# Hybrid decoder trunk on one core: combining the experts' rows on TensorE and VectorE, and computing the position tables during the router

## Chip, cores and metric

The kernel runs on one core of a Trainium2 chip. The time is that of one execution on the device, in microseconds (us). Median before the change: 1937.03 us of 3 runs (1935.52 to 1939.13).

## What is computed

A trunk of two layers over 512 tokens of 1024 float32 values: layer 0 is an RWKV-7 time mix and a mixture of experts, layer 1 a sparse attention (NSA) with a shared key/value side and position bias, and a second mixture of experts; then a last norm. The change touches the mixtures of experts and the bias tables. In words of the reference, cut:

```python
def hier_moe(h, ln_g, w_gr, b_gr, w_er, b_er, w1, w3, w2):
    xf = rms_norm(h, ln_g)
    ...            # one of 4 groups, then 2 of its 8 experts per token
    weight = grp_w * ew / jnp.sum(ew, -1, keepdims=True)
    ...
    # per expert: (silu(xb @ w1[e]) * (xb @ w3[e])) @ w2[e], hidden size 512
    y = zeros.at[buf_t].add(yb * buf_w)      # each token: weighted sum of two rows
    return y
# the caller adds y to h
table = rel_bias.reshape(REL_BUCKETS, G, HPG).transpose(1, 2, 0)
logits = q @ k * scale + table[:, :, rel_bucket(distance)]
```

## The kernel before

The engines run hand-written instruction streams, ordered by semaphores; each stream is in order. SBUF is one arena of twelve regions of 4096 floats per partition; `h`, the residual stream, is region 0, as four blocks `j` of 128 tokens.

**Experts.** `moe_loads` lets SyncE load each of 32 experts' weights, w13 (4 MB, L375) and w2 (2 MB, L380), into one of three slots of three regions, as soon as TensorE has left the slot. In layer 0, w13(1), w2(1) and w13(2) are issued when the output product of the time mix is done (`wo_mm`), and w2(2) after `h_rwkv` = 8, since its region 5 held `x_again` until then. The router (L1763 places the tokens, L1766 counts them, after VectorE's chain up to `two_hot`, L1142) gives each token two experts. An expert holds 64 rows: `gather` (16 matmuls with a one-hot matrix), `hidden` (16 matmuls of 512 columns), ScalarE's silu (L744), VectorE's product (L1223), `transpose_gated` (L1792), VectorE's copy (L1232), `result` (8 matmuls), ScalarE's copy to `yb` (L750), and GpSimd's indirect DMA of these rows to `y_rows` in DRAM (L513).

**Combine.** When the stores of all 32 experts have landed, GpSimd gathers for each block `j` and each of its two choices `c` the rows by eight indirect DMAs (L544) to `y_got`; `combine` lets VectorE add them, weighted, to `h` (L1269, two a block). Then a block's norm: ScalarE's square (L568), VectorE's variance (L882), ScalarE's root (L573), VectorE's reciprocal (L887) and scaling (L892), TensorE's eight transposes (`turn_block`, L1412), and copies with the gain by VectorE (`turned`, L898) and ScalarE (L579). After layer 0 the q projection follows (w_qg), the gate product, and the K/V units (w_kv). After layer 1 a last scaling (L1397) and the store of the output follow. Of an expert with more than 64 tokens, the rest goes through the overflow branch (`n_over`), which the profiled execution does not enter.

**Position tables.** After layer 0's experts TensorE computes the bias tables from one-hot buckets: 55 matmuls for `bias_c` and two for the reversed rows. ScalarE copies them out (L768 to L771); SyncE later writes the reversed rows 128-fold to `rev_bias` in DRAM (L444), ahead of the second compression weights cmp_v_w1 (L446), and reads them back as `bias_h`. All matmuls are recorded at the helper lines `mm` (L1404) and `transpose` by their own lines; a float32 matmul is two instructions in the trace, a transpose one.

```python
                if l == 0:
                    sp.wait_ge(sem("h_rwkv"), 8)
                w2(2)
```

## Time and profile before

| | |
|---|---|
| median of 3 runs | 1937.03 us |
| profiled execution | 1936.99 us |
| its span | 1935.2 us |
| TensorE busy | 1811.9 us (94%) |
| VectorE, ScalarE, GpSimd busy | 596.3, 360.5, 219.7 us |
| mean granted TensorE clock | 0.96 |
| DMA | 499.73 MB, mean 258 GB/s |

PE is TensorE, DVE VectorE, ACT ScalarE, POOL GpSimd, SP SyncE. PEclk is the granted clock of TensorE as a share of 2.4 GHz, so 0.50 is 1.2 GHz. Times inside the trace count from the span's start.

### The profile page before, as it was taken

The numbers are of one execution on the slowest core, as the hardware profiler recorded it, in microseconds if no ns is written. First come the engines' busy times: TensorE is split into PE (matmuls) and PEld (weight loads), VectorE is DVE, ScalarE is ACT, GpSimd is POOL, SyncE is SP. The second block draws the span as 40 slices with busy tenths as digits, with TensorE's granted clock in tenths as the row PEclk, the third lists the DMA queues.
The fourth block names the chain that finished last, engine by engine and source line by source line (L and its number), as shares of the span: only waits on it lengthen the run. The fifth ranks groups of instructions, "written<-read, shape, count | busy, mean of one in ns | idle before, by whom it ended". The sixth has DMA issues, their size and how long they took to land.

```text
span 1935.2 us, 25676 instructions
## 1 busy us (share of the span) xinstructions
PE 1811.9 (94%) x10954; PEld 956.7 (49%) x10954; DVE 596.3 (31%) x1269; ACT 360.5 (19%) x846; POOL 219.7 (11%) x264
## 2 busy tenths in 40 slices
PE   7989988989799999999969999999979999999993
PEld 3334347755554454445434577555554544454440
DVE  5462793452221111111140335564222111111113
ACT  2432113311100000000030123665210000000001
POOL 2044000000000000000020001453000000000002
PEclk9989998999799999999969999999979999999997
DMA  5112743060899999999959302010379999999994
GB/s 206 63 68 50 276 123 49 3 269 1 347 416 432 428 426 430 430 430 428 422 220 167 68 22 109 13 34 1 131 298 407 431 431 428 428 430 429 429 404 153
DMA packets 60930, 499.73 MB, mean 258 GB/s; under 512 B 28079, under 2 KB 28591, under 8 KB 42383
## 3 DMA queue, kind: packets, MB, share of 16 engines
q1 hardware_dynamic: 53391, 481.26, 62.1%
q0 software_dynamic: 7424, 16.80, 2.4%
q8 instruction: 89, 1.46, 0.3%
q14 instruction: 26, 0.21, 0.0%
HBM read 465.23 MB, written 41.18 MB: 262 GB/s over the span
## 4 chain that ended last, share of the span: by engine, by line
PE 84%; DVE 8%; issue 3%; DMA 3%; POOL 1%; ACT 1%; SPq 0%; POOLq 0%; DVEq 0%; ACTq 0%
PE bank L1404 71%; PE bank L1456 5%; PE bank L1987 3%; PE bank L2001 2%; DVE spare L1017 2%; DVE arena L1018 1%; PE bank L1792 1%; DVE arena L1269 1%; DMA arena<-y_rows,ints 1%; POOL arena L493 1%; DMA arena<-gram_dram 1%; POOL arena L491 0%; PE bank L1412 0%; DVE arena L1031 0%; PE bank L1564 0%
## 5 line engine op out<-in xcount | busy, mean ns | idle before, releaser
L1404 PE MATMUL bank<-arena 128*64 128x512 f32 (+8 forms) x5090 | 1255.8, 546 | 26.2 <-DVE arena L982 9.5
L1404 PEld LDWEIGHTS bank<-arena 128*64 128x64 f32 (+4 forms) x5090 | 482.6, 156 | 676.4 <-issue 653.3
L1404 PEld LDWEIGHTS bank<-const,arena 128*128 128x128 f32 x2048 | 238.9, 195 | 51.2 <-issue 48.7
L1404 PE MATMUL bank<-const,arena 128*128 128x128 f32 x2048 | 250.7, 282 | 2.2 <-DVE const L1148 2.2
L513 POOL DMA_INDIRECT y_rows<-arena,ints x64 | 63.1, 986 | 1124.4 <-ACT arena L750 923.5
L1223 DVE TENSOR_TENSOR arena<-arena,bank 128x256 f32<-128x256 f32 x64 | 27.0, 421 | 426.6 <-ACT arena L744 426.6
L750 ACT ACTIVATE arena<-bank 128x512 f32<-128x512 f32 x64 | 38.3, 598 | 424.2 <-PE bank L1404 424.2
L744 ACT ACTIVATE arena<-bank 128x256 f32<-128x256 f32 x64 | 24.6, 385 | 469.2 <-PE bank L1404 469.2
L1155 DVE TENSOR_TENSOR arena<-bank,vec 128x512 f32<-128x512 f32 x64 | 44.3, 692 | 193.3 <-PE bank L1404 193.3
L560 POOL TENSOR_SCALAR arena<-arena,small 128x128 f32<-128x128 f32 (+3 forms) x128 | 77.0, 612 | 143.7 <-DVE small L1381 143.2
L1232 DVE COPY arena<-bank 128x256 f32<-128x256 f32 x64 | 27.2, 424 | 184.3 <-PE bank L1792 184.3
L1456 PE MATMUL bank<-arena 128*64 128x64 f32 (+2 forms) x1760 | 65.9, 231 | 10.6 <-DVE arena L1031 5.4
L851 ACT ACTIVATE arena<-arena,small 128x128 f32<-128x128 f32 (+3 forms) x128 | 70.5, 552 | 25.9 <-DVE small L1373 25.8
L1456 PEld LDWEIGHTS bank<-arena 128*64 128x64 f32 (+2 forms) x1760 | 59.8, 143 | 17.1 <-DVE arena L1031 6.2
L1373 DVE CUSTOM_DVE_ANT_0 arena<-bank,arena 128x128 f32<-128x128 f32 (+3 forms) x128 | 58.0, 489 | 23.3 <-PE bank L1404 22.3
L1987 PE MATMUL bank<-const,arena 128*128 128x128 f32 x320 | 62.7, 294 | 0.7 <-POOL arena L560 0.6
L1987 PEld LDWEIGHTS bank<-const,arena 128*128 128x128 f32 x320 | 34.4, 140 | 40.3 <-POOL arena L560 24.6
L2001 PE MATMUL bank<-arena 128*64 128x128 f32 x640 | 49.1, 282 | 0.4 <-DVE arena L1388 0.4
L927 DVE SCALAR_TENSOR_TENSOR arena<-arena,vec 128x512 f32<-128x512 f32 x48 | 36.9, 797 | 39.4 <-PE bank L1404 34.9
L1388 DVE COPY arena<-bank 128x128 f32<-128x128 f32 (+3 forms) x64 | 31.1, 486 | 42.9 <-PE bank L1987 42.6
L1017 DVE TENSOR_TENSOR spare<-arena 128x529 f32<-128x529 f32 (+30 forms) x40 | 43.1, 1078 | 1.4
L2001 PEld LDWEIGHTS bank<-arena 128*64 128x64 f32 x640 | 33.9, 136 | 16.3 <-issue 9.3
(239 smaller groups left out, 981.5 us busy)
## 6 DMA issues: line engine op xcount, KB each, us to landing
arena<-m_w SPq DMA_DIRECT2D x64, 4096.0 KB, 18.5
arena<-m_w SPq DMA_DIRECT2D x64, 2048.0 KB, 17.2
y_rows<-state SPq DMA_DIRECT2D x1, 8192.0 KB, 22.6
arena<-kv_w SPq DMA_DIRECT2D x1, 6144.0 KB, 18.4
rev_bias<-arena SPq DMA_DIRECT2D x1, 5120.0 KB, 70.1
arena<-a_wk SPq DMA_DIRECT2D x2, 2048.0 KB, 15.1
arena<-a_wr SPq DMA_DIRECT2D x2, 2048.0 KB, 8.0
arena<-a_wv SPq DMA_DIRECT2D x2, 2048.0 KB, 8.0
```

The costliest lines, as they stand in the source:

```text
L513: nc.gpsimd.indirect_dma_start(out=y_halves, out_offset=bass.IndirectOffsetOnAxis(ap=store_i[:, e:e + 1], axis=0), in_=yb[:, n % 2, :], in ...
L560: nc.gpsimd.tensor_scalar(row, row, share[:, n % 4, i:i + 1], gates[:, j, g:g + 1], ALU.mult, ALU.mult).then_inc(sem("shared"), 1)
L750: nc.scalar.activation(yb[:, n % 2, :], bank[6 + n % 2][:, :], ACT.Copy).then_inc(sem("yb_ready"), 1)
L851: last = nc.scalar.activation(probs[:, n % 4, i, 0:P * (j + 1)], probs[:, n % 4, i, 0:P * (j + 1)], ACT.Exp, scale=-1.0, bias=top[:, n % 4 ...
L927: return nc.vector.scalar_tensor_tensor(dst[:, k, :], xxT[:, k, :], v8(f"mu{mu}")[:, k:k + 1], xT[:, k, :], ALU.mult, ALU.add)
L1017: solved(nc.vector.tensor_tensor(prod, known, below, ALU.mult))
L1155: nc.vector.tensor_tensor(xgT[:, n % 2, 4 * q:4 * q + 4, :], bank[2 + q][:, :].rearrange("p (k t) -> p k t", k=4), spread(gain[:, 4 * q:4 ...
L1373: last = nc.vector.tensor_tensor_reduce(out=probs[:, n % 4, i, 0:P * (j + 1)], in0=bank[2 * (n % 2) + i][:, 0:P * (j + 1)], in1=bias_h(m)[ ...
L1404: return nc.tensor.matmul(dst, lhsT, rhs, start=start, stop=stop)
L1456: return nc.tensor.matmul(dst, lhsT, rhs, start=start, stop=True, skip_group_check=True)
L1987: last = nc.tensor.transpose(bank[4 + i][:, P * s:P * s + P], probs[:, n % 4, i, P * s:P * s + P], ident)
L2001: last = nc.tensor.matmul(bank[6 + m % 2][64 * i:64 * i + 64, P * j:P * j + P], values[:, s, b, HD * (m // 2):HD * (m // 2) + HD], probs_T ...
```

## The change

- **The last two experts** (30 and 31) are not stored and gathered. VectorE writes, in expert 29 (`tail_picks`), weighted one-hot matrices of both; TensorE transposes them (`tail_turn`, eight transposes) within expert 30, ScalarE copies them to `tail_T`. After the last expert `tail_add(j)` multiplies them with `yb` in SBUF: four matmuls a block, each with 64 rows, into banks 2j and 2j + 1.
- **The other thirty** are gathered once the stores up to expert 29 have landed (`EARLY` = 30), to regions 3 and 4. VectorE sums them (`early_sum`), except for block 2 (layer 0) and blocks 1 and 2 (layer 1), where TensorE adds them with diagonal matrices (`early_add`, four matmuls). VectorE then adds both banks to `h`.
- **The position tables** of layer 0 are computed in the router, before the tokens are placed: SyncE loads buckets and `rel_bias` between w13(2) and w2(2), TensorE does four matmuls (three of 512 columns, one of 128) into 16 partitions, ScalarE copies, SyncE stores them to DRAM, and w2(2) waits for the store. `bias_c` is later read from there by eight DMAs, and `rev_bias` is written from DRAM.
- **The scaling** of the norm after layer 0 moves from VectorE to ScalarE. Weight slots are counted by `e % 3`; overflow has buffers of its own; several tiles change regions; w_qg is loaded in halves and w_kv in thirds.

The diff, cut to these parts:

```diff
@@ -392,6 +406,12 @@
                 w13(2)
                 if l == 0:
                     sp.wait_ge(sem("h_rwkv"), 8)
+                    sp.dma_start(fwd, d["bucket_fwd"]).then_inc(sem("bucket_in"), 16)
+                    sp.dma_start(rev, d["bucket_rev"]).then_inc(sem("bucket_in"), 16)
+                    sp.dma_start(rel[0:32, :], d["rel_bias"]).then_inc(sem("bucket_in"), 16)
+                    sp.wait_ge(sem("bias_ev"), at("bias_ev", 4))
+                    sp.dma_start(bias_dram, bias_rows).then_inc(sem("bias_out"), 16)
+                    sp.wait_ge(sem("bias_out"), at("bias_out", 16))
...
 
-            sp.wait_ge(sem("hidden_mm"), at("hidden_mm", E - 2))
-            sp.dma_start(w_qg[:, 0:7, :], d["b_wqg"][:, 0:7, :]).then_inc(sem("q_w_in"), 16)
-            sp.wait_ge(sem("expert_mm"), at("expert_mm", E - 2))
-            for i in range(2):
-                sp.dma_start(fwd[i], d["bucket_fwd"]).then_inc(sem("bias_in"), 16)
-                sp.dma_start(rev[i], d["bucket_rev"]).then_inc(sem("bias_in"), 16)
-                sp.dma_start(rel[i][0:32, :], d["rel_bias"]).then_inc(sem("bias_in"), 16)
-            sp.dma_start(w_qg[:, 7, :], d["b_wqg"][:, 7, :]).then_inc(sem("q_w_in"), 16)
+            sp.wait_ge(sem("hidden_mm"), at("hidden_mm", E - 1))
+            sp.dma_start(w_qg[:, 0:4, :], d["b_wqg"][:, 0:4, :]).then_inc(sem("q_w_in"), 16)
+            sp.wait_ge(sem("expert_mm"), at("expert_mm", E - 1))
+            sp.wait_ge(sem("y_got1"), 32)
+            sp.dma_start(w_qg[:, 4:NK, :], d["b_wqg"][:, 4:NK, :]).then_inc(sem("q_w_in"), 16)
             overflow_sp(0)
             sp.wait_ge(sem("combined"), 8)
-            sp.dma_start(w_kv, d["kv_w"]).then_inc(sem("kv_w_in"), 16)
+            for i in range(3):
+                sp.dma_start(w_kv[i], d["kv_w"][:, i, :, :]).then_inc(sem("kv_w_in"), 16)
+            for a in range(8):
+                sp.dma_start(bias_c[16 * a:16 * a + 16, :, :],
+                             bass.AP(tensor=bias_dram.tensor, offset=9 - a, ap=[[64, 16], [1664, NH], [1, NOFF]])
+                             ).then_inc(sem("bias_c_in"), 16)
             sp.dma_start(cmp_w1[0], d["cmp_k_w1"]).then_inc(sem("cmp_w1_in0"), 16)
             sp.dma_start(cmp_w2[0], d["cmp_k_w2x2"].rearrange("(s p) n -> p s n", p=P)).then_inc(sem("cmp_w2_in"), 16)
             sp.dma_start(cmp_w2[1], d["cmp_v_w2"].rearrange("(s p) n -> p s n", p=P)).then_inc(sem("cmp_w2_in"), 16)
             for i in range(2):
                 sp.dma_start(cmp_pe[i], d["pe_k" if i == 0 else "pe_v"]).then_inc(sem("cmp_pe_in"), 16)
-            sp.wait_ge(sem("rev_ev"), at("rev_ev", 1))
-            sp.dma_start(rev_dram, spread(rev_rows, 1, P)).then_inc(sem("rev_out"), 16)
+            sp.dma_start(rev_dram, spread(bias_dram[:, 1024:1664], 1, P)).then_inc(sem("rev_out"), 16)
             sp.wait_ge(sem("gate_mm"), at("gate_mm", 1))
...
                         bounds_check=2 * SLOTS - 1, oob_is_err=False).then_inc(sem(f"y_store{n % 2}"), 16)
 
                 pool.wait_ge(sem("entries_ready"), at("entries_ready", l + 1))
+                for i in range(2):
+                    pool.wait_ge(sem(f"y_store{i}"), 16 * (EARLY // 2) * (l + 1))
+                pool.wait_ge(sem("hidden_mm"), at("hidden_mm", E * l + EARLY))
+                for j in range(NJ):
+                    for c in range(2):
+                        nc.gpsimd.indirect_dma_start(
+                            out=y_got[:, j, c, :], out_offset=None, in_=y_rows,
...
                 nc.scalar.activation(grp4, grp4, ACT.Exp).then_inc(sem("group_exp"), 1)
+                if l == 0:
+                    act.wait_ge(sem("bias_mm"), at("bias_mm", 4))
+                    for i, (a, b, sign) in enumerate(((0, 512, 1.0), (512, 1024, 1.0), (1024, 1536, -1.0), (1536, 1664, -1.0))):
+                        nc.scalar.activation(bias_rows[:, a:b], bank[(6, 7, 0, 1)[i]][0:NH, 0:b - a], ACT.Copy,
+                                             scale=sign).then_inc(sem("bias_ev"), 1)
                 act.wait_ge(sem("top_diff"), at("top_diff", l + 1))
                 nc.scalar.activation(e21, e21, ACT.Exp).then_inc(sem("top_exp"), 1)
...
                         nc.scalar.activation(yb[:, n % 2, :], bank[6 + n % 2][:, :], ACT.Copy).then_inc(sem("yb_ready"), 1)
+                        if e == EARLY - 1:
+                            for i in range(2):
+                                act.wait_ge(sem("tail_mm"), at("tail_mm", 2 * l + i + 1))
+                                nc.scalar.activation(tail_T[:, i, :, :].rearrange("p j t -> p (j t)"), bank[2 + i][:, :],
+                                                     ACT.Copy).then_inc(sem("tail_turned"), 1)
                 n_over = act.value_load(over_count, min_val=0, max_val=OVER)
                 with act.If(n_over > 0):
                     with act.Fori(0, n_over) as b:
...
             nc.scalar.activation(root_warm, gn_eps, ACT.Sqrt)
             for j in range(NJ + 2):
                 if 1 <= j <= NJ:
                     norm_root(2, j - 1)
+                    act.wait_ge(sem("norm_rstd"), 4 * 2 + j - 1 - 3)
+                    nc.scalar.activation(xn_m[:, j - 1, :], h[:, j - 1, :], ACT.Copy,
+                                         scale=rstd[:, j - 1:j]).then_inc(sem("xn_ready"), 1)
                 if j < NJ:
```

```diff
+                def tail_picks():
+                    for c, hot in enumerate((hot1, hot2)):
+                        to = tail_f if c else tail_w
+                        then(nc.vector.tensor_tensor(to, hot[:, :, EARLY:E], spread(combine_w[:, :, c], 2, 2), ALU.mult))
+                    then(nc.vector.tensor_tensor(tail_w, tail_w, tail_f, ALU.add))
+                    dve.wait_ge(sem("gathered_T"), at("gathered_T", 32 * (l + 1)))
+                    for i in range(2):
+                        tile = one_hot[:, i, :, :, :]
+                        then(nc.vector.tensor_tensor(tile, spread(spread(cst("iota")[:, 1:CAP + 1], 1, 2), 1, NJ),
+                                                     spread(spread(place_of[:, :, EARLY + i], 2, 2), 3, CAP), ALU.is_equal))
+                        nc.vector.tensor_tensor(tile, tile, spread(spread(tail_w[:, :, i], 2, 2), 3, CAP),
+                                                ALU.mult).then_inc(sem("tail_hot"), 1)
+                    lo = by_pe[l][0]
+                    n = 2 * len(by_pe[l])
+                    nc.vector.tensor_tensor(early_diag[:, 0:n, :], spread(ident, 1, n),
+                                            spread(small[:, 464 + 2 * lo:464 + 2 * lo + n], 2, P), ALU.mult).then_inc(sem("diag_ready"), 1)
 
                 dve.wait_ge(sem("place_mm"), at("place_mm", l + 1))
...
+
+            early_sums = [0]
+
+            def early_sum(l, j):
                 dve.wait_ge(sem(f"y_got{j}"), 32 * (l + 1))
                 for c in range(2):
-                    if c:
-                        dve.wait_ge(sem("combined"), 8 * l + 2 * j + 1)
-                    nc.vector.scalar_tensor_tensor(h[:, j, :], y_got[:, j, c, :], combine_w[:, j, c:c + 1], h[:, j, :],
-                                                   ALU.mult, ALU.add).then_inc(sem("combined"), 1)
+                    nc.vector.scalar_tensor_tensor(h[:, j, :], y_got[:, j, c, :], early_w[:, j, c:c + 1], h[:, j, :],
+                                                   ALU.mult, ALU.add).then_inc(sem("early_sum"), 1)
+                    early_sums[0] += 1
+                    dve.wait_ge(sem("early_sum"), at("early_sum", early_sums[0]))
+
+            def combine(l, j):
+                if j not in by_pe[l]:
+                    early_sum(l, j)
+                dve.wait_ge(sem(f"tail_out{j}"), at(f"tail_out{j}", l + 1))
+                for q in range(2):
+                    cols = slice(512 * q, 512 * q + 512)
+                    nc.vector.tensor_tensor(h[:, j, cols], bank[2 * j + q][:, :], h[:, j, cols],
+                                            ALU.add).then_inc(sem("combined"), 1)
 
             moe_dve(0)
...
                     combine(0, j)
                 if 1 <= j <= NJ:
                     norm_var(2, j - 1)
-                    norm_scale(2, j - 1)
+                    dve.wait_ge(sem("norm_std"), 4 * 2 + j - 1 - 3)
+                    nc.vector.reciprocal(rstd[:, j - 1:j], rstd[:, j - 1:j]).then_inc(sem("norm_rstd"), 1)
...
 
+                if l == 0:
+                    pe.wait_ge(sem("bucket_in"), at("bucket_in", 48))
+                    pe.wait_ge(sem("rel_mask"), at("rel_mask", 1))
+                    for b, table in ((6, fwd[:, 0:512]), (7, fwd[:, 512:1024]), (0, rev[:, 0:512]), (1, rev[:, 512:640])):
+                        mm(bank[b][0:NH, 0:table.shape[1]], rel, table).then_inc(sem("bias_mm"), 1)
                 pe.wait_ge(sem("two_hot"), at("two_hot", l + 1))
...
+
+                def tail_turn(i):
+                    pe.wait_ge(sem("tail_hot"), at("tail_hot", 2 * l + i + 1))
+                    for j in range(NJ):
+                        last = nc.tensor.transpose(bank[2 + i][:, P * j:P * j + P],
+                                                   one_hot[:, i, j, :, :].rearrange("p e t -> p (e t)"), ident)
+                    last.then_inc(sem("tail_mm"), 1)
+
+                def tail_add(j):
+                    for i in range(2):
+                        for q in range(2):
+                            rows = slice(CAP * q, CAP * q + CAP)
+                            last = mm(bank[2 * j + q][:, :], tail_T[rows, i, j, :], yb[rows, i, :], i == 0, i == 1 and j not in by_pe[l])
+                    if j not in by_pe[l]:
+                        last.then_inc(sem(f"tail_out{j}"), 1)
+
+                def early_add(j):
+                    pe.wait_ge(sem(f"y_got{j}"), 32 * (l + 1))
+                    for q in range(2):
+                        for c in range(2):
+                            last = mm(bank[2 * j + q][:, :], early_diag[:, 2 * by_pe[l].index(j) + c, :],
+                                      y_got[:, j, c, 512 * q:512 * q + 512], False, c == 1)
+                    last.then_inc(sem(f"tail_out{j}"), 1)
 
...
                     if e:
                         expert_result(e - 1)
+                    if e == EARLY:
+                        for i in range(2):
+                            tail_turn(i)
                     pe.wait_ge(sem("gated_ready"), at("gated_ready", n + 1))
+                    if n == 0:
+                        pe.wait_ge(sem("bias_ev"), at("bias_ev", 4))
...
+                tail_add(0)
+                if l == 0:
+                    tail_add(1)
+                    tail_add(3)
+                    tail_add(2)
+                    early_add(2)
+                else:
+                    tail_add(1)
+                    early_add(1)
+                    tail_add(2)
+                    early_add(2)
+                    tail_add(3)
 
             moe_pe(0)
 
-            pe.wait_ge(sem("bias_in"), at("bias_in", 96))
-            pe.wait_ge(sem("rel_mask"), at("rel_mask", 1))
-            for m in range(NOFF):
-                mm(bank[m % 2][:, 16 * (m // 2):16 * (m // 2) + 16], fwd[m % 2][:, 864 - 16 * m:992 - 16 * m], rel[m % 2])
-            mm(bank[3][0:NH, 0:128], rel[1], rev[1][:, 512:640])
-            mm(bank[2][0:NH, :], rel[0], rev[0][:, 0:512]).then_inc(sem("bias_mm"), 1)
-            pe.wait_ge(sem("rev_ev"), at("rev_ev", 1))
             for j in range(NJ):
                 turn_block(2, j, 2 * j)
```

## Rows read from the trace of the kernel before

**Rows 1.** Windows view; columns: stretch, length, busy (instructions) by engine, PEclk, DMA share, GB/s.

```profile
513.30:978.00 464.70, 464.14 (x2568) 221.01 (x2568) 66.75 (x154) 31.12 (x64) 30.60 (x31) 1.00 0.98 414
978.00:1011.00 33.00, 16.87 (x145) 13.53 (x143) 18.05 (x27) 12.97 (x37) 8.96 (x10) 0.57 0.55 203
```

**Rows 2.** Chain of waits, layer 0's last expert on; columns: start us, us, what.

```profile
974.03 3.68 PE bank L1404 x16
977.73 0.61 ACT arena L750
...
986.20 7.09 DMA arena<-y_rows,ints
...
1010.86 1.19 PE bank L1404
```

**Rows 3.** Chain of waits, the kernel's end.

```profile
1899.20 3.68 PE bank L1404 x16
...
1930.85 1.28 DVE arena L1397
```

**Rows 4.** Chain of waits, layer 0's router.

```profile
498.58 0.21 DVE spare L1142
...
502.29 10.28 PE bank L1404 x64
```

**Rows 5.** Source view of w13's load line, the load issued at 484.3.

```profile
L375 SPq DMA_DIRECT2D arena<-m_w x1: 432/432/432, 484.3 to 484.3; - x1
...
DMA to landing us min/median/max: 26.4/26.4/26.4
```

**Rows 6.** DMA issues of SyncE's queue, 405 to 413; columns: KB each, median us to landing.

```profile
arena<-x SPq DMA_DIRECT2D x1, 2048.0 KB, 12.2
...
state<-router_b SPq DMA_DIRECT2D x1, 36.0 KB, 12.0
```

**Rows 7.** Groups by form, 978 to 1011; columns: busy, mean ns | idle before.

```profile
L1269 DVE SCALAR_TENSOR_TENSOR arena<-arena,small 128x1024 f32<-128x1024 f32 x8 | 10.3, 1283 | 16.6 <-DMA arena<-y_rows,ints 16.5
L1412 PE MATMUL bank<-const,arena 128*128 128x128 f32 x32 | 7.8, 426 | 14.9 <-DVE arena L892 14.9
...
L579 ACT ACTIVATE arena<-bank,vec 128x128 f32<-128x128 f32 x18 | 5.0, 367 | 1.9 <-PE bank L1412 1.9
L898 DVE TENSOR_TENSOR arena<-bank,vec 128x512 f32<-128x512 f32 x7 | 4.5, 684 | 0.6 <-PE bank L1412 0.6
L568 ACT ACTIVATE arena<-arena 128x1024 f32<-128x1024 f32 x4 | 4.2, 1044 | 1.4 <-DVE arena L1269 1.4
...
L1404 PE MATMUL bank<-arena 33*16 33x512 f32 x2 | 1.9, 1044 | 0.0
...
L1404 PE MATMUL bank<-arena 33*16 33x128 f32 x2 | 0.6, 404 | 0.0
```

**Rows 8.** Windows view, short stretches for TensorE's granted clock.

```profile
502.00:506.00 4.00, 3.71 (x17) 3.71 (x18) 0.54 (x3) 0.00 (x0) 0.00 (x0) 0.50 1.06 459
...
508.00:509.00 1.00, 1.00 (x9) 1.00 (x9) 0.00 (x0) 0.00 (x0) 0.00 (x0) 0.84 1.06 459
...
982.00:984.00 2.00, 2.00 (x30) 2.00 (x29) 0.00 (x0) 0.00 (x0) 1.31 (x2) 0.69 0.00 0
```

**Rows 9.** The page's costliest groups, the gather's matmul.

```profile
L1404 PE MATMUL bank<-const,arena 128*128 128x128 f32 x2048 | 250.7, 282 | 2.2 <-DVE const L1148 2.2
```

**Rows 10.** Source view of the expert store's line, the store issued at 963.8.

```profile
L513 POOL DMA_INDIRECT y_rows<-arena,ints x1: 972/972/972, 963.8 to 963.8; - x1
...
DMA to landing us min/median/max: 10.8/10.8/10.8
```

**Rows 11.** TensorE groups by form, 1192 to 1389.

```profile
L1404 PE MATMUL bank<-arena 128*128 128x512 f32 x96 | 42.0, 593 | 0.0
L1404 PE MATMUL bank<-arena 64*128 64x512 f32 x64 | 18.1, 641 | 0.0
```

**Rows 12.** Windows view, the stretch in which rev_bias is broadcast.

```profile
1030.00:1050.00 20.00, 20.00 (x48) 8.76 (x48) 0.69 (x1) 1.19 (x2) 0.00 (x0) 1.00 0.95 100
```

More of the change, by code:

```diff
@@ L244, in decoder_program @@
         combine_w = small[:, 88:96].rearrange("p (j c) -> p j c", c=2)
+        early_w, over_w, tail_w = (small[:, 464 + 8 * i:472 + 8 * i].rearrange("p (j c) -> p j c", c=2) for i in range(3))
         slot_i = ints[:, 0:8].rearrange("p (j c) -> p j c", c=2)
+        over_slot_i = ints[:, 176:184].rearrange("p (j c) -> p j c", c=2)
+        is_early, tail_f = scratch(NJ * 2), scratch(NJ, 2)
         entry_i = ints[:, 8:16].rearrange("p (j c) -> p j c", c=2)
@@ L306, in decoder_program @@
         NU = len(UNITS)
-        final_gain = region(3)[:, 0:D]
+        final_gain = region(7)[:, 0:D]
         block = stack.enter_context(nc.Block())
@@ L509, in moe_pool @@
                 pool.wait_ge(sem("store_rows"), l + 1)
-                for e in range(E):
+                for e in range(EARLY):
                     n = E * l + e
@@ L1112, in moe_dve @@
                     add(j)
+                    if l == 0 and j == NJ - 1:
+                        dve.wait_ge(sem("h_rwkv"), 8)
+                        nc.vector.memset(rel[32:33, :], NEG).then_inc(sem("rel_mask"), 1)
                     norm_var(i, j)
@@ L1262, in moe_dve @@
                         dve.wait_ge(sem(f"over_store{l}"), 32 * b + 32)
-            def combine(l, j):
+                    dve.wait_ge(sem(f"over_got{l}"), 128)
+                    for j in range(NJ):
+                        for c in range(2):
+                            then_over(nc.vector.scalar_tensor_tensor(h[:, j, :], over_got[:, j, c, :], over_w[:, j, c:c + 1], h[:, j, :],
+                                                                     ALU.mult, ALU.add))
+            early_sums = [0]
```

188 lines of the change are left out of this document (104 added, 84 removed), and 2 rows, old and new, of the table GOES_ON.

## The prediction

> **What bounds the kernel now.** I read the busy time by stretches first [rows 1]. In the first mixture-of-experts stretch TensorE is busy 464.14 of 464.70 us at full clock. What the change can win or lose there shows only when TensorE itself gains work or waits. In the 33.00 us after it, which the stretch view shows from 978 to 1011, TensorE is busy only 16.87 us. The chain of waits says why [rows 2]: the last expert's matmuls start at 974.03 and end 3.68 us later (977.71), then come ScalarE's copy, the store of its rows, a gather that lands after 7.09 us, the sums and norms, and the q projection only at 1010.86. That is a gap of 33.15 us. At the end of the kernel it is the same [rows 3]: matmuls end at 1902.88, VectorE's last instruction at 1930.85 + 1.28 = 1932.13, 29.25 us later, and 3.07 us of output store follow. These two gaps are what the change attacks.
>
> The third place is the router before the first experts. There the chain goes through VectorE to TensorE: two_hot is written at 498.58 + 0.21 = 498.79, after which TensorE places the tokens and begins gathering at 502.29 [rows 4]. The change puts a wait and four matmuls of TensorE just ahead of that placing.
>
> **Part 1, the tables in the router's wait (layer 0).** SyncE now issues the three table loads after w13(2) and ahead of w2(2); they can't go earlier, since region 5 holds x_again until h_rwkv. I look at what stands ahead of them. w13(2) is issued at 484.3 and lands 26.4 us later, at 510.7 [rows 5], because w13(1) and w2(1), issued in the microsecond before, go first. Do small transfers pass large ones in this queue? Earlier, the router's 36 KB bias, issued behind the 2 MB reload of x, took 12.0 us, against x's own 12.2: it landed with the large one, 1/57 of its size [rows 6]. I read this as one queue in order. So the tables (132 + 82.5 + 2 KB, some 0.5 us at the stretch's 414 GB/s) land near 511.2. TensorE's new wait for bucket_in holds everything behind it in order: the placing, the first gather, the first expert. It could have gone on at 498.79, so the stall is 12.4 us. What VectorE's router chain hides (TensorE idle until 498.84) is already used up by then.
>
> Then come four table matmuls, on the path. Of this shape the old kernel ran one with 512 columns, two instructions in 1.9 us, and one with 128 columns, 0.6 us, both at the low clock [rows 7]; three and one cost 3 x 1.9 + 0.6 = 6.3 us. ScalarE's four evacuations are covered by placing and gathering (over 10 us); the store of the tables and its round trip only delay w2(2), which is needed two experts later, and w13(3) waits for the first expert anyway. Part 1 adds 12.4 + 6.3 = **18.7 us**. The 57 matmuls removed after the experts save nothing: they lay in the 33 us gap, which ended by the gather.
>
> Clock: it stood at 0.50 from 502 to 506, and rose within 508 to 509, under the wide gather matmuls; and within 982 to 984 it fell to a mean of 0.69 while TensorE was busy all the time with the old narrow table matmuls [rows 8]. So I count on no help from narrow matmuls. Bounds: nothing, or the gather of 10.28 us [rows 4] at full clock, where the 2048 of its form take 250.7 / 2048 = 0.122 us each, 64 of them 7.8 us [rows 9]: 2.5 us less. I take nothing.
>
> **Part 2, the combine after layer 0.** TensorE gains eight transposes for the tail (tail_turn), within expert 30: in this stretch eight take 7.8 / 4 = 2.0 us at the low clock [rows 7], half of it, 1.0, at full: **+1.0 us** a layer, since TensorE is the bound there. VectorE's picks fall into its idle time. The gathers move: the store of expert 29 starts about where one did before (963.8) and that one landed after 10.8 us beside weight loads [rows 10]; I let this one land by 971 to 975, since less is queued, and the eight gathers, an issue of about 1.3 us each, between 978 and 991. The w_qg half now waits for y_got1, is 2.2 MB, so about 5 us, and is there well before its use.
>
> From the last expert matmul (+0), the new chain: copy 0.6; tail_add(0), four matmuls with 64 rows, 64 instructions of that form take 18.1 us [rows 11], so 0.565 us a matmul, 2.26 in all: +2.9. VectorE adds two halves of block 0 at 0.69 each (a PSUM operand, 4.5 / 7 in the row, rounded up) [rows 7]: +4.3. TensorE goes on with three more tail_adds and early_add(2), four matmuls with 128 rows at 2 x 42.0 / 96 = 0.875: 2.9 + 6.8 + 3.5 = +13.1. VectorE's block 1 needs two sums (1.28 each) and two adds: +8.3. Block 2 waits for TensorE: +14.5. Then block 1's norm steps and a turned copy (1.3), two sums and two adds of block 3: +19.8. Now ScalarE, which has taken over the scaling, is last: per block a scaling (1.04, at its square's price), a square with its read (1.25), a turned copy (1.14): after scaling(2) +21.3, square(3) +22.6, turned(1) +23.7, scaling(3) +25.2; transposes at the low clock (2.0) +27.2, the last turned copy **+28.4**. Against 33.15 that gains 4.7 us, far less than the earlier landing of the rows: what the DMA no longer holds, VectorE's 19.8 us and then ScalarE do.
>
> **Part 3, the combine after layer 1.** TensorE: tail0 +2.9, tail1 and early1 +8.6, tail2 and early2 +14.3, tail3 +16.6. VectorE: block 0 +4.3, block 1 waits, +10.0, its neighbour's norm and final product (1.9) +11.9; block 2 waits, +15.7, final +17.6; block 3 with sums and adds (4.0) +21.6; two finals +25.2. Before 29.25: gain 4.0 us.
>
> **Other parts, at nothing.** Six more small operations in entries() (0.2 to 0.3 us each) lie under expert 4; renamed regions and slots keep the order of frees. The position table now reaches bias_c by DMA, and the broadcast to rev_bias reads DRAM. The old broadcast ran at 100 GB/s with the DMA 0.95 busy [rows 12], 5.24 MB in some 50 us, and cmp_v_w1 is queued behind it when the gate product is done; before its user, the second compression product, come six K/V units of 8 x 0.875 = 7.0 us, 42 us of slack. At the old rate it is hidden; if that cover goes, rival (d) has the price.
>
> **Sum.** 18.7 + 2 x 1.0 - 4.7 - 4.0 = +12.0 us. The profiled execution took 1936.99 us (span 1935.2; the rest lies around it), the median shown is 1937.03, the same. Forecast 1936.99 + 12.0 = **1949.0 us**, slower.
>
> **Rivals.**
> (a) The tables don't queue (the other side): the first table load is issued near 485; if it lands before 493, the 6.3 us of matmuls fill TensorE's idle 6.1 us ahead of 498.84 and Part 1 costs 0.2. Then 1936.99 + 0.2 + 2.0 - 8.7 = 1930.5 us. It decides if small transfers pass w13(1) to w13(2); against it stand the transfers of [rows 6]. The whole change breaks even at a landing near 499. 13%.
> (b) The table matmuls wake the clock. In rows: the 2.5 us of above come back, 1946.5 us. For: the clock rose under the wide matmuls of the gather [rows 8]; against: it fell under narrow ones. 13%.
> By the Trainium skill (TensorE: Matmul & The Clock Gate, Part 1, what's actually happening) the low clock is the default and sustained activity releases it; by that rule (b) would hold, since the table matmuls are activity ahead of the gather. The trace agrees for wide matmuls, and disagrees for the narrow ones of 982 to 984.
> (c) The 64-row halves don't share the array here, 0.875 a matmul instead of 0.565: 16 of them. Every tail_add is 1.24 longer and the chains above become 33.1 and 28.8: gains 0.1 and 0.5, so 1936.99 + 18.7 + 2.0 - 0.6 = 1957.1 us. For: unlike the scores, two of them accumulate in turn on one bank. Against: each pair has its own rows and bank. 10%.
> (d) The broadcast from DRAM, or 2048 runs of 220 bytes ahead of it, delay cmp_v_w1 by over 40 us: above 1958 us, 4%.
>
> **How the numbers follow.** The forecast's own case has 60%, from 1943 to 1954 (a table landing 1 to 4 us later, gathers delayed, combine chains off by 2 us each). The range 1941 to 1958 takes in (b) and (c) and leaves out (a), (d) and a little, under 20%. What a measurement can tell from no change is 0.2%, 3.9 us. Faster: nearly all of (a), 0.12. Same: 0.05, a table landing half way or larger combine gains. Slower 0.83.
>
> **What would show it.** Right: TensorE idle from 493 to about 511 in the router, released by the bucket DMA; the placing near 517.5; the first gather near 521. After the experts, the q projection 28.4 us after the last expert matmul, with VectorE waiting for TensorE at block 2 and ScalarE busy to the end; at the kernel's end 25.2 us to VectorE's last. Wrong: bucket_in landing before 500, a placing near 499, or gaps under 20 us after the experts.

## The result, and the profile after

The changed kernel took 1951.14 us (median of 8 executions, 1946.03 to 1964.67), the kernel before 1937.19 us beside it (8 executions, 1934.65 to 1942.92): ratio 1.0075, 95% interval 1.0059 to 1.0092. It is slower by 14.0 us by the medians; the forecast was 12.0. Two later repeats gave less: +7.9 and +12.5 us (e4_after_again and e10_after_third below).

| | before | after |
|---|---|---|
| median | 1937.19 us | 1951.14 us |
| profiled execution, its span | 1936.99, 1935.2 us | 1964.67, 1961.9 us |
| TensorE busy | 1811.9 us (94%) | 1854.0 us (95%) |
| mean granted TensorE clock | 0.96 | 0.956 |

The profiled execution of after is the slowest of its eight. One plain reason lies far ahead of the change's code, in the time mix. In both fences here, the windows view, the columns are those of [rows 1]; first after, then before:

```profile
201.00:262.00 61.00, 60.01 (x95) 20.68 (x96) 52.90 (x69) 6.91 (x12) 0.95 (x1) 0.72 0.53 195
```

```profile
200.00:262.00 62.00, 61.70 (x138) 24.76 (x137) 54.88 (x70) 6.78 (x12) 0.95 (x1) 1.00 0.67 222
```

TensorE is as busy in both, but the granted clock is 0.72 in one and 1.00 in the other. The output product of the time mix ends at 496.10 and not 483.43, 12.7 us later. The low clock isn't the change's: e3_before_plus_tables, the kernel before with a few instructions behind this point, shows the same 0.72 and its product ends 10.5 us late (493.92). In all the other profiles the clock is not low here, and still this product ends anywhere from 483.1 to 485.7 us. So I read distances inside the trace, not times from its start.

**The router.** Before (chain of waits), from the end of the output product to the placing is 15.4 us, and to the first expert (513.34, in the stretch of [rows 1]) 29.9:

```profile
476.55 6.88 PE bank L1404 x16
...
498.84 0.80 PE bank L1763 x2
```

After, the same chain of waits:

```profile
489.22 6.88 PE bank L1486 x16
...
498.44 25.98 DMA arena<-rel_bias
...
524.47 5.72 PE bank L1486 x8
530.19 0.72 PE bank L1850 x2
...
533.57 9.66 PE bank L1486 x64
...
544.01 10.86 PE bank L1486 x64
```

VectorE has left the chain. It runs through SyncE's issues to the load of rel_bias, last of the three tables, which lands 28.3 us after the product. Then come the table matmuls (5.72 us), the placing, and the gather of 64, which answers to [rows 4] and is a little shorter. The first expert starts 47.9 us after the product, where it was 29.9: +18.0.

**After the experts, layer 0** (chain of waits, answers to [rows 2]):

```profile
1005.57 3.65 PE bank L1486 x16
1009.23 2.22 issue
1011.45 12.48 PE bank L1486 x40
1023.95 1.29 DVE arena L1349 x2
...
1030.68 1.15 ACT arena L810
...
1038.66 3.75 PE bank L1486 x4
```

The DMA that held this chain in [rows 2] is gone: TensorE's 40 instructions are the tail and the diagonal products (four tail_adds, early_add(2)). VectorE waits for them at block 2 (L1349), then ScalarE's scaling (L810), squares and turned copies are last. From the end of the last expert matmul (1009.22) to the q projection it takes 29.4 us (before 33.15), with 2.22 us in which TensorE issues nothing.

**The end** (chain of waits, answers to [rows 3]): 24.25 us from 1934.59 to 1958.83, before 29.25.

```profile
1930.67 3.92 PE bank L1486 x16
...
1935.35 12.90 PE bank L1486 x40
1948.27 1.29 DVE arena L1349 x2
...
1957.55 1.28 DVE arena L1479
```

### The profile page after: what moved, and what is told of

Its sections match the earlier page's. It is cut to its first block, busy times and chain, and to the rows that moved or that the text cites. A ratio compares the mean times of both kernels' runs of the same rounds, so it can differ in the third digit from the quotient of the medians.

```text
span 1961.9 us, 25727 instructions
## 1 busy us (share of the span) xinstructions
PE 1854.0 (95%) x10952; PEld 965.9 (49%) x10952; DVE 602.8 (31%) x1304; ACT 366.9 (19%) x854; POOL 214.8 (11%) x260
## 4 chain that ended last, share of the span: by engine, by line
PE 93%; DVE 3%; DMA 2%; issue 1%; ACT 1%; SPq 0%; POOL 0%; DVEq 0%; PEldq 0%; POOLq 0%; ACTq 0%
PE bank L1486 80%; PE bank L1538 5%; PE bank L2111 3%; PE bank L2125 2%; DMA arena<-rel_bias 1%; PE bank L1879 1%; DVE arena L1066 1%; PE bank L1494 1%; PE bank L1646 0%; PE bank L2119 0%; DMA arena<-x 0%; PE bank L1501 0%; DVE arena L1349 0%; DVE arena L1009 0%; DVE arena L1338 0%
## 5 line engine op out<-in xcount | busy, mean ns | idle before, releaser
L1486 PE MATMUL bank<-arena 128*64 128x512 f32 (+9 forms) x5008 | 1272.0, 555 | 44.7 <-DMA arena<-rel_bias 19.1
L886 ACT ACTIVATE arena<-arena,small 128x128 f32<-128x128 f32 (+3 forms) x128 | 70.4, 552 | 25.9 <-DVE small L1455 25.8
L1538 PE MATMUL bank<-arena 128*64 128x64 f32 (+2 forms) x1760 | 61.8, 223 | 9.7 <-DVE arena L1066 7.3
L1455 DVE CUSTOM_DVE_ANT_0 arena<-bank,arena 128x128 f32<-128x128 f32 (+3 forms) x128 | 57.6, 488 | 23.3 <-PE bank L1486 22.3
L1486 PE MATMUL bank<-state,arena 128*128 128x36 f32 (+2 forms) x160 | 49.2, 467 | 3.7 <-ACT arena L607 2.5
## 6 DMA issues: line engine op xcount, KB each, us to landing
arena<-kv_w SPq DMA_DIRECT2D x3, 2048.0 KB, 12.3
arena<-b_wqg SPq DMA_DIRECT2D x2, 2144.0 KB, 10.5
```

Source lines behind the costliest of these rows:

```text
L886: last = nc.scalar.activation(probs[:, n % 4, i, 0:P * (j + 1)], probs[:, n % 4, i, 0:P * (j + 1)], ACT.Exp, scale=-1.0, bias=top[:, n % 4 ...
L1455: last = nc.vector.tensor_tensor_reduce(out=probs[:, n % 4, i, 0:P * (j + 1)], in0=bank[2 * (n % 2) + i][:, 0:P * (j + 1)], in1=bias_h(m)[ ...
L1486: return nc.tensor.matmul(dst, lhsT, rhs, start=start, stop=stop)
L1538: return nc.tensor.matmul(dst, lhsT, rhs, start=start, stop=True, skip_group_check=True)
```

## The experiments

Each run is read at three distances in us, from its chain of waits: router (end of the output product to the first expert, before 29.9), layer 0 (last expert matmul to the q projection, 33.15) and end (last expert matmul to VectorE's last, 29.25). The theories at stake: the cost lies in the order of SyncE's queue (the forecast's), against a cost in the new matmuls or in the combine itself. The table has the distances that the argument uses.

| run | median us | ratio to the kernel before, 95% interval | router | layer 0 | end |
|---|---|---|---|---|---|
| e1_tables_first | 1928.04 | 0.9961 (0.9943 to 0.998) | 29.9 | 26.3 | 24.25 |
| e2_tables_mid | 1930.99 | 0.9977 (0.9954 to 1.0) | 34.3 | | |
| e3_before_plus_tables | 1958.46 | 1.0098 (1.0072 to 1.0124) | 48.5 | | |
| e4_after_again | 1945.35 | 1.0035 (1.0019 to 1.0051) | 48.1 | 26.3 | 24.25 |
| e5_sum_in_wait | 1928.18 | 0.9964 (0.9949 to 0.9979) | | 28.4 | 21.6 |
| e6_scale_dve | 1927.76 | 0.9948 (0.9926 to 0.9969) | | 25.3 | |
| e7_both | 1924.50 | 0.9941 (0.9919 to 0.9962) | | 26.35 | 21.6 |
| e8_wqg_after_rows | 1924.66 | 0.9932 (0.991 to 0.9954) | | 25.9 | 21.85 |
| e9_one_block_pe | 1923.26 | 0.9942 (0.9922 to 0.9962) | | 23.5 | 20.3 |
| e10_after_third | 1948.91 | 1.0054 (1.0036 to 1.0071) | 47.8 | 27.4 | 24.25 |
| e11_no_overflow_branch | 1930.95 | 0.9968 (0.9954 to 0.9983) | | 26.9 | |

The kernel before, run beside them, had medians of 1937.41 (e1 to e4), 1936.79 (e5 to e7), 1936.42 (e8, e9) and 1936.36 us (e10, e11).

**e1_tables_first**: the change, with the table loads and the wait for h_rwkv ahead of the weights.

```diff
-                w13(1)
-                w2(1)
-                w13(2)
-                if l == 0:
                     sp.wait_ge(sem("h_rwkv"), 8)
...
                     sp.dma_start(rel[0:32, :], d["rel_bias"]).then_inc(sem("bucket_in"), 16)
+                w13(1)
+                w2(1)
+                w13(2)
+                if l == 0:
                     sp.wait_ge(sem("bias_ev"), at("bias_ev", 4))
```

> The changed kernel with one thing moved: SyncE issues the three table loads ahead of w13(1), w2(1) and w13(2) (after the same h_rwkv = 8), not behind them. Theory (one queue in order, 10 MB ahead): the tables land 2 to 4 us after their issue, about 487 on the clock of the trace before, the four matmuls (5.7 us in the changed kernel's profile) run in TensorE's router wait, and the placing starts 16 us after the last output product instead of 34.8: the router's cost of 18.0 us falls to 0.5 or so, the median from 1951 to about 1933, 4 us under the kernel before. Rival (the wait was for something else in these small loads, such as their shape or the h_rwkv wait itself): the placing stays more than 25 us after the output product and the median over 1945.

Its chain of waits has the old router again:

```profile
476.26 6.88 PE bank L1486 x16
...
498.64 0.80 PE bank L1850 x2
...
502.09 10.15 PE bank L1486 x64
...
513.01 10.86 PE bank L1486 x64
```

The placing stands at 498.64 as it did at 498.84 before: tables that land early, and four matmuls, cost nothing while TensorE waits for VectorE. By medians it is 9.4 us faster than before, where I expected 4, and 17.3 us faster than the changed kernel in the same comparison (1945.35, e4). The distances give 33.15 - 26.3 + 29.25 - 24.25 - 2.0 = 9.9 us, with 2.0 for the two tail_turns.

**e2_tables_mid**: the loads between w13(1) and w2(1).

```diff
                 w13(1)
-                w2(1)
-                w13(2)
                 if l == 0:
...
                     sp.dma_start(rel[0:32, :], d["rel_bias"]).then_inc(sem("bucket_in"), 16)
+                w2(1)
+                w13(2)
+                if l == 0:
```

> As before, but the table loads stand behind w13(1) alone, ahead of w2(1) and w13(2). Theory: they land just after w13(1), about 13.5 us after the last output product (w13(1) landed 12.6 us after its issue), the matmuls end near 19.5 us after it, against 15.4 us when the placing could start: the router costs 4 us, the median about 1937. Rival: no dose, the same as with the tables behind everything, or the same as with them first.

```profile
485.62 13.55 DMA arena<-rel_bias
499.21 5.72 PE bank L1487 x8
```

Behind 4 MB, not 10, the same tables land 15.0 us after the product (484.12 to 499.17), not 28 to 29, and the router takes 4.4 us more than before; I expected 4. The median is 3.0 us over e1's, not the 1937 that I expected, since I had taken e1 too slow as well. The landing follows what is queued ahead: these small loads do not pass the large ones here.

**e3_before_plus_tables**: the kernel before with nothing of the new combine; it only loads the tables behind w13(2) and multiplies them, and no one uses the products.

```diff
                     sp.wait_ge(sem("h_rwkv"), 8)
+                    sp.dma_start(region(5)[0:33, 0:1024], d["bucket_fwd"]).then_inc(sem("extra_in"), 16)
+                    sp.dma_start(region(5)[0:33, 1024:1664], d["bucket_rev"]).then_inc(sem("extra_in"), 16)
+                    sp.dma_start(region(5)[0:32, 1664:1680], d["rel_bias"]).then_inc(sem("extra_in"), 16)
+                    sp.wait_ge(sem("extra_mm"), 1)
                 w2(2)
...
+                if l == 0:
+                    pe.wait_ge(sem("extra_in"), 48)
+                    for b, lo, n in ((6, 0, 512), (7, 512, 512), (0, 1024, 512), (1, 1536, 128)):
+                        last = mm(bank[b][0:NH, 0:n], region(5)[0:32, 1664:1680], region(5)[0:32, lo:lo + n])
+                    last.then_inc(sem("extra_mm"), 1)
```

> The kernel before, with only the router part added: the three loads between w13(2) and w2(2), TensorE's wait and four matmuls ahead of the placing, and w2(2) waiting for these matmuls. Nothing is done with their results, and the old tables are still computed later. Theory (the router part alone is the loss): +18.0 us, about 1955 against 1937, with no other stretch changed. Rival (the loss needs the rest of the change, as the store to DRAM and its round trip): under +10 us.

```profile
487.04 6.88 PE bank L1408 x16
...
496.15 27.11 DMA arena<-rel_bias
...
542.38 2.79 PE bank L1408 x11
```

The router takes 48.5 us: its whole loss comes with this part alone. The median is of less use than the trace: of four executions two took 1953.4 and 1953.7 (+16 us), two 1963.2 and 1965.7, and the profiled one, the slowest, shows the low clock at 200 to 262 us again.

**e4_after_again**: the changed kernel, unedited, in the same comparison as e1 to e3.

> The changed kernel unchanged, as the reference on this chip, and to see whether its runs spread again from 1946 to 1965 us. The profiled one (1964.67) was already 12.6 us late when the time mix ended, with a clock of 0.72 in a stretch of 61 us in which TensorE was busy. Theory: that is the chip's clock in single runs and none of the change's; the median is about 1951, and a profile at full clock there has a span near 1948. Rival: the delay returns in each profile of this kernel, then it belongs to the change.

The delay did not return: all eight executions took 1943.4 to 1947.6 us, less than the 1951 that I expected. The profiled one has no low stretch in the time mix and can be read line against line. Its groups by form around the table matmuls and after the last expert:

```profile
L1486 PE MATMUL bank<-arena 33*16 33x512 f32 x6 | 5.3, 1052 | 19.7 <-DMA arena<-rel_bias 19.7
...
L1486 PE MATMUL bank<-arena,const 64*128 64x512 f32 x32 | 7.1, 595 | 0.8 <-ACT arena L783 0.8
```

And its windows view for the clock:

```profile
514.00:520.00 6.00, 5.82 (x9) 1.17 (x10) 0.00 (x0) 0.06 (x1) 0.00 (x0) 0.50 0.00 0
520.00:525.00 5.00, 3.89 (x18) 3.75 (x19) 1.28 (x4) 3.02 (x6) 0.00 (x0) 0.50 0.25 38
525.00:527.00 2.00, 2.00 (x12) 2.00 (x12) 0.00 (x0) 0.00 (x0) 0.00 (x0) 0.54 0.83 287
527.00:529.00 2.00, 2.00 (x21) 2.00 (x20) 0.09 (x1) 0.00 (x0) 0.00 (x0) 1.00 0.98 418
```

The account by distances is 18.2 (router) + 2.0 (two tail_turns, 1.02 us each) - 6.9 (layer 0) - 5.0 (end) = +8.3 us; the medians say +7.9 (3.7 to 9.9 by the interval).

**e5_sum_in_wait** (on e1): VectorE adds block 3's gathered rows while it waits for TensorE at the first block that TensorE sums.

```diff
-                if j not in by_pe[l]:
+                if j == by_pe[l][0]:
+                    early_sum(l, 3)
+                if j not in by_pe[l] and j != 3:
                     early_sum(l, j)
```

> e1 (tables first), with VectorE's two sums for block 3 moved to the place where it waits for TensorE: ahead of block 2's adds after layer 0, ahead of block 1's after layer 1. In e1's profile VectorE's last instruction comes 24.25 us after the last expert matmul of layer 1, and the q projection 26.27 us after that of layer 0. Theory (VectorE's order sets the end of the kernel, ScalarE's chain that after layer 0): the first falls by the two sums, 2.5 us, to 21.7; the second by only about 1.2 us, to 25, since ScalarE then still has its scaling, square and copies in a row. Rival 1 (VectorE sets both): 2.5 us at both. Rival 2 (the gathered rows of block 3 aren't there yet): no gain, VectorE waits for y_got3.

The end came as expected (24.25 to 21.6). Layer 0 got worse, 28.4 us, and the median gains nothing (1928.18, e1 1928.04); the chain of waits says that the sum now comes before its rows are there, so rival 2 holds in layer 0:

```profile
979.81 11.20 DMA arena<-y_rows,ints
...
991.03 1.30 DVE arena L1338
```

**e6_scale_dve** (on e1): the scaling back on VectorE (`norm_scale`), ScalarE keeps squares, roots and copies.

```diff
-                    act.wait_ge(sem("norm_rstd"), 4 * 2 + j - 1 - 3)
-                    nc.scalar.activation(xn_m[:, j - 1, :], h[:, j - 1, :], ACT.Copy,
-                                         scale=rstd[:, j - 1:j]).then_inc(sem("xn_ready"), 1)
...
-                    dve.wait_ge(sem("norm_std"), 4 * 2 + j - 1 - 3)
-                    nc.vector.reciprocal(rstd[:, j - 1:j], rstd[:, j - 1:j]).then_inc(sem("norm_rstd"), 1)
+                    norm_scale(2, j - 1)
```

> e1, with the scaling of the norm after layer 0 back on VectorE (0.76 us a block in the kernel before, against 1.15 on ScalarE). Theory (ScalarE is the last chain there): the q projection comes about 2 us earlier than e1's 26.27 us, near 24.5, nothing else moves. Rival (VectorE is the last chain, and gets 0.76 us a block more): 1 to 3 us later.

Layer 0 takes 25.3 us, 1.0 better where I expected 2: ScalarE did stand last, but with VectorE loaded again the chain soon goes through both by turns.

**e7_both**: the edits of e5 and e6 together.

> e1 with both edits of e5 and e6. Theory: after layer 0 they add up to more than their sum, since VectorE's idle time is filled and ScalarE is freed: the q projection 4 us earlier than in e1, near 22.3 us after the last expert matmul; at the kernel's end 2.5 us as in e5. The median goes from e1's 1928.0 to about 1921.5. Rival (one chain hides the other, so only the larger counts): 1923.5 to 1925.

It is 12.3 us faster than the kernel before, and 1924.50 where I expected 1921.5. Layer 0 stays at 26.35 (22.3 expected), held by the same landing:

```profile
978.69 12.47 DMA arena<-y_rows,ints
...
991.18 1.29 DVE arena L1335
```

**e8_wqg_after_rows** (on e7): what delays that gather? SyncE issues 2.2 MB of w_qg at 979.6, 0.9 us after it. Here it waits for the last block's rows.

```diff
-            sp.wait_ge(sem("y_got1"), 32)
+            sp.wait_ge(sem("y_got3"), 32)
             sp.dma_start(w_qg[:, 4:NK, :], d["b_wqg"][:, 4:NK, :]).then_inc(sem("q_w_in"), 16)
```

> e7 with one wait changed: SyncE holds the second half of w_qg (2.2 MB) until y_got3 instead of y_got1, so that the last rows don't share the DMA engines with it. In e7 the last gather was issued at 978.69 and landed 12.5 us later (991.18), VectorE waiting 3.7 us for it, and the q projection came 26.35 us after the last expert matmul, where 22.3 were expected. Theory (contention with w_qg kept block 3's rows back): they land 6 to 8 us after the issue, VectorE waits for nothing, the q projection comes near 23 us, the median is about 3 us under e7's 1924.5. w_qg lands near 994, before its use. Rival (the gathers themselves need that long, 2 MB through one queue): no change, or later by what w_qg is late.

The source view of the gathers' line, all sixteen, in e7 and then in e8:

```profile
L545 POOL DMA_INDIRECT arena<-y_rows,ints x16: 933/951/1646, 969.6 to 1895.8; - x16
...
DMA to landing us min/median/max: 4.3/6.2/12.5
```

```profile
L545 POOL DMA_INDIRECT arena<-y_rows,ints x16: 937/954/1737, 970.9 to 1898.5; - x16
...
DMA to landing us min/median/max: 6.4/6.6/6.8
```

The long landing is gone, and with it VectorE's wait for these rows: holding this load back is the only edit, so its traffic was the cause. The median did not follow, 1924.66 where I expected some 1921.5; against the kernel before beside them, e7 and e8 are 12.3 and 11.8 us faster. In the profile layer 0 gains 0.5 us (25.9), because this one has TensorE's late start again, 2.20 us:

```profile
975.66 3.65 PE bank L1484 x16
979.32 2.20 issue
981.51 12.48 PE bank L1484 x40
```

The 40 instructions take 12.48 us here and 10.78 in e4, at a clock that was 0.50 from 982 to 985. Without these 1.7 us and the late start it is the 23 that I expected: the next run, whose code is the same in layer 0, has 23.5. Why the executions as a whole don't show it is open.

**e9_one_block_pe** (on e8): TensorE sums one block in layer 1 too, not two, and its order there becomes that of layer 0.

```diff
-        by_pe = ((2,), (1, 2))
+        by_pe = ((2,), (2,))
```

> e8, with block 1 of layer 1 summed by VectorE as in layer 0, and TensorE's order there the same (tails of 0, 1, 3, 2, then the diagonal products of block 2): four matmuls of 128 rows (3.5 us) less on TensorE, two sums (2.6 us) more on VectorE. In e5's profile VectorE waits 1.4 + 2.4 us there for gathered rows and TensorE and its last instruction comes 21.6 us after the last expert matmul. Theory (TensorE's chain of adds is what VectorE waits for): that falls to about 20.2, the median by 1.4 us against e8. Rival (VectorE is the bound of this stretch once its sums are moved): later by 1 to 2.6 us.

The end is 20.3 us (1897.12 to 1917.39), as expected. That counts from the chain's end of the last matmul; in the timeline this matmul ends 1.0 us earlier and ScalarE's copy, which everything else follows, starts late, at 1897.14. From copy to VectorE's last it is 20.25 us, in e8 21.6. At 1923.26 us e9 has the lowest median here, 13.2 us below the kernel before and 1.4 below e8, but against e7 and e8 the intervals don't separate it. Its layer 0 (23.5) is not this edit's doing.

**e10_after_third**: the changed kernel once more.

> The changed kernel once more, on another chip, since the two comparisons so far differ: +14.0 us by the medians of the first, +7.9 us in e4_after_again. My account by stretches gives 18.2 + 2.0 - 6.9 - 5.0 = +8.3 us, and +11.4 where TensorE starts the tail after layer 0 late by 2.2 us and then runs it slower, as in the first profile. Theory 1 (the account is whole, the first comparison had more executions with dips of TensorE's clock): +7 to +10 us by the medians, 1943 to 1948. Theory 2 (the account misses a cost of the change that e4's executions happened to lack): +12 to +15 us, 1949 to 1952.

By the medians, +12.5 us, it falls at the lower edge of Theory 2; the interval, +7.0 to +13.7, allows both. Its distances give 17.9 + 2.0 - 5.8 - 5.0 = +9.1, but the spans differ by 11.7 (1946.9 and 1935.2). The account by distances is thus not complete; where the rest lies is shown under "Sum" below.

**e11_no_overflow_branch** (on e1): TensorE's branch for overflowing tokens is taken out; that part of the computation is left out.

```diff
-                n_over = pe.value_load(over_count, min_val=0, max_val=OVER)
-                with pe.If(n_over > 0):
...
                 pe.wait_ge(sem("tail_turned"), at("tail_turned", 2 * l + 2))
```

> e1_tables_first without TensorE's branch for tokens beyond the experts' slots, which stands between the last expert's matmuls and the first tail product (it leaves out that part of the computation; for this input no token takes it). Theory 1 (the 2.2 us in which TensorE issues nothing there in some profiles belongs to that branch, its register load and jump): the tail product starts 0.14 us after ScalarE's copy in every profile, and where e1_tables_first pays the gap in some executions the median falls by up to 1 us, 1927 to 1928. Theory 2 (the gap has another cause): it may show here too, 2.2 us between the last expert matmul and the tail product, and the median is e1_tables_first's, 1928.0. A profile without the gap doesn't tell the two apart, one with it does.

The gap is there without the branch (1.34 us, timeline of e11; columns: start us, us, engine, line, operation, idle before):

```profile
979.65 0.60 ACT L783 ACTIVATE arena<-bank 128x512 f32<-128x512 f32 x1 [4.50 <-PE bank L1486]
...
980.39 1.99 PE L1486 MATMUL bank<-arena,const 64*128 64x512 f32 x8 [1.34 <-issue]
```

In e1 TensorE's expert matmuls end at 978.25 and ScalarE's copy starts at 978.27:

```profile
978.27 0.60 ACT L783 ACTIVATE arena<-bank 128x512 f32<-128x512 f32 x1 [3.94 <-PE bank L1486]
```

In e11 they end at 979.05 and the copy starts at 979.65. So it is the copy that is late, by 0.6 us here and by 1.1 to 1.5 us in e10_after_third, e8 and after; TensorE only follows 0.15 us behind it, with the branch or without. Theory 1 fell. The median, 1930.95, is above what either theory gave. Why the copy starts late in some executions is open; the profile models the ends of matmuls, so a matmul that in truth ended late would look the same.

## Why the prediction was right

**Part 1, right.** The three tables landed with what stood ahead of them, 28.3 (after), 28.5 (e10) and 29.1 us (e4) after the output product; I had 27.8 (511.2 against 483.43). The stall is thus 12.9 to 13.7 us, not 12.4; the four matmuls took 5.72, not 6.3; the gather 9.1 to 9.7, not 10.28. The sum is +17.9 to +18.2 against 18.7. e3 shows this part alone, e1 that only the order in SyncE's queue makes it cost. tail_turn took 1.02 us a layer (forecast 1.0).

**Part 2, mechanism right, size off by 2 us.** VectorE waits for TensorE at block 2, then ScalarE is last, as forecast. The term that was mis-sized is the matmul with 64 rows: 0.565 us in the forecast (18.1 / 32 from [rows 11]), 7.1 / 16 = 0.444 in e4. Over 16 matmuls that is 1.9 us. TensorE's part ended 11.5 us after the last expert matmul in e4, not 13.1, and VectorE's steps from there to the end of block 3 took 0.4 less than I gave them: together nearly all of the 2.1 by which e4's 26.3 lies under 28.4. In e8 and after, where TensorE had first waited 2.2 us for ScalarE's late copy, its 40 instructions took 12.48 us, not 10.78. The windows view of after shows the clock there:

```profile
1009.00:1011.00 2.00, 0.23 (x2) 0.00 (x0) 0.95 (x1) 0.30 (x1) 1.70 (x3) 1.00 0.97 350
...
1013.00:1015.00 2.00, 2.00 (x8) 1.08 (x6) 0.90 (x2) 0.10 (x1) 0.00 (x0) 0.50 1.08 442
1015.00:1018.00 3.00, 3.00 (x14) 1.36 (x12) 2.93 (x4) 1.15 (x2) 0.00 (x0) 0.81 1.04 431
```

The clock fell to 0.50 soon after TensorE had gone on (1011.45), and rose again within 1015 to 1018. It stayed at 1.00 in e10 and e11, where TensorE had waited too (1.86 and 1.34 us). So layer 0 took 29.4 us in that execution and 26.3 in e4 and e1: 1.5 us more by the late copy and 1.7 by the low clock. Counted from ScalarE's copy to the q projection, e1, e4, e10 and e11 agree: 26.25 to 26.26 us.

**Part 3, mechanism right.** The end took 24.25 us in all four profiles (after, e1, e4, e10) against 25.2. Most of it is the same term again: three tails run before VectorE's wait at block 2, which ended 13.7 us after the last expert matmul in e4, not 14.3.

**Sum.** The forecast was +12.0 of 18.7 + 2.0 - 8.7; the distances give +8.3 (e4), +9.1 (e10) and +11.3 (after: 18.0 + 2.0 - 3.7 - 5.0). The comparisons gave +7.9, +12.5 and +14.0. The median on record, 1951.14, is 2.1 us from the forecast; that closeness is partly luck: by e4 the change costs 3.7 us less than I took, 3.2 of it because the combine gained more (11.9 against 8.7), and other executions are longer for reasons that I didn't forecast. The spans, cut into all their stretches (us, from the chains of waits), show where these lie:

| | before | e1 | e4 | e10 | after |
|---|---|---|---|---|---|
| to the end of the time mix's output product | 483.4 | 483.1 | 485.1 | 485.7 | 496.1 |
| router | 29.9 | 29.9 | 48.1 | 47.8 | 47.9 |
| experts of layer 0 | 464.4 | 465.2 | 465.2 | 465.2 | 465.2 |
| layer 0, to the q projection | 33.15 | 26.3 | 26.3 | 27.4 | 29.4 |
| q projection to the last expert matmul of layer 1 | 892.0 | 892.4 | 892.1 | 893.5 | 895.9 |
| end, to VectorE's last | 29.25 | 24.25 | 24.25 | 24.25 | 24.25 |

The first row is ahead of the change, and 3.1 us of output store follow the last in each. In the fifth, e10 has 1.5 us and after 3.9 us more than before; about 1.0 of these is the second tail_turn's, and in after the clock was low once more, at 0.50 from about 1429 to 1433 us, where its output product and transposes took 1.7 us more than e4's. What else makes the first and the fifth row differ no run explains. Outside the span an execution of after took 2.1 to 3.1 us more, one of before 1.8. The other seven executions of the first comparison have no trace, so what made up their +14.0 us is open.

**Rivals.** (a) fell: the tables queue. e1 is what it described, 1928.04 us against its 1930.5, got by another order of the issues. (c) fell: 0.444 us a matmul. (Its own sum for layer 0 is 0.3 us low: 28.4 + 4 x 1.24 is 33.4.) (d) fell: after 1036 us no wait of TensorE in the profile of after names a DMA, and the longest is VectorE's 6.1 us in the second router. (b) is not settled. The clock stayed at 0.50 all through the table matmuls (e4's windows above), so they didn't wake it themselves. Once the gather had begun it rose sooner: a full 1.00 from 527, 3.7 us after the start at 523.28, while in [rows 8] it was still rising 6 us after 502.29. The gather took 9.1 to 9.7 us in the five profiles with table matmuls right ahead of it (after, e2, e3, e4, e10), 0.6 to 1.2 us less than before. Of the eight profiles without them seven have 10.15 to 10.28, but e8 has 8.82, and the same gather of layer 1, which no run puts table matmuls ahead of, takes 8.8 to 10.4. So some gain from the table matmuls fits these rows and isn't shown by them.
By the Trainium skill (TensorE: Matmul & The Clock Gate, Part 1, what's actually happening), sustained activity releases the clock. The trace of e4 agrees in that the rise came within the added and the following work (a full 1.00 from 527), but the clock still read 0.50 when the table matmuls ended at 519.90; that they brought the rise forward is not shown.

What I named at no cost and was not free: the w_qg half. I said it is there well before its use, which holds, but its traffic stretched a gather to 12.5 us (e7), where with the load held back none took over 6.8 (e8). In the change that gather is as long (11.5 us at most in after) and nobody waits for it; e5 and e7 made it matter.

## What to carry to other kernels

A small load on the critical path goes ahead of the large prefetches in its queue; ask of each wait that is added what bytes stand in front of it. Here 216 KB behind 10 MB cost 18 us in the router and turned a change that gains 9.4 us (e1) into a loss. When work is moved from one engine to another, look again at who is last: here it went from DMA to TensorE, ScalarE and VectorE in turn, and the four edits behind e1 brought only some 4 us more (e9, -13.2 us against the kernel before beside it). And cut a span into all its stretches before calling an account complete: the profiles of e4 and after, one and the same kernel, differ by 3.8 us in a stretch that the account by distances left out.

## What was unexpected of the hardware

- A matmul of 64 rows and 512 columns took 0.444 us in pairs after the experts (e4), 0.565 in the scores of [rows 11]. No run says why.
- In some executions ScalarE starts a copy 0.5 to 1.5 us after the end that the profile gives the matmul that releases it (at 979.65 for 979.05 in e11). The gathers are in flight then, but so they are in e1 and e4, where it starts at once. Nothing in the profile says why.
- The granted clock stood at 0.72 for some 60 us in the midst of busy TensorE work in two profiles (after and e3), which goes with a product that ends 10 to 13 us late. Some executions of the kernel before (1943.9 to 1946.8 us beside e1, with a mean clock of 0.953 to 0.955 against 0.96) may have it too; none of them has a trace.
- The eight loads of bias_c (2048 runs of 220 bytes in all) kept SyncE 14.7 us in issue (one took 7.9), off the path here (e4):

```profile
L457 SPq DMA_DIRECT2D spare<-bias_rows x8: 448/510/7919, 1017.5 to 1031.7; - x8
```
